# Delta rule of a hybrid block: inverse, u product and state update on four quarters of the array

## The chip, the cores and the metric

The kernel runs as one program on one core of a Trainium2 chip. The metric is the device time in microseconds (us) of one execution; lower is better. Two kernels, before and after one change, are compared. The engines are called as in the profile: PE (TensorE), DVE (VectorE), ACT (ScalarE), POOL (GpSimd) and SP (the queue that issues most DMAs).

## The reference, cut to what matters

The program computes several transformer blocks in one launch. The change lies in one branch of the first block, the gated delta rule, over 256 positions, 4 heads of 128 and chunks of 64 positions:

```python
def gated_deltanet(...):                       # B=1, S=256, H=4, dk=128, C=64, N=4 chunks
    ...
    kb = k * beta[..., None]
    lower = jnp.where(strict, jnp.einsum("bhnid,bhnjd->bhnij", kb, k) * decay, 0.0)
    rhs = jnp.concatenate([v * beta[..., None], kb * jnp.exp(gc)[..., None]], axis=-1)
    sol = lax.linalg.triangular_solve(lower + jnp.eye(C), rhs,
                                      left_side=True, lower=True, unit_diagonal=True)
    u, w = jnp.split(sol, 2, axis=-1)
    ...
    def step(state, xs):
        q_i, k_i, u_i, w_i, a_i, gl_i = xs
        v_new = u_i - jnp.einsum("bhcd,bhde->bhce", w_i, state)
        o_i = jnp.einsum("bhcd,bhde->bhce", q_i, state) + jnp.einsum("bhij,bhje->bhie", a_i, v_new)
        state = state * gl_i[..., None, None] + jnp.einsum("bhcd,bhce->bhde", k_i, v_new)
        return state, o_i
```

So 16 unit lower triangular matrices of 64x64 (4 heads by 4 chunks) are inverted and applied to two right sides, and a scan over the 4 chunks carries a 128x128 state for each head.

## The kernel before, in words

**Weights.** Everything hangs on one stream of weight products. A *unit* is two times 128 rows of a weight matrix, up to 512 columns wide, 512 KB. SP loads it into `raw` (5 slots), ACT writes its high half `whi` (L613), POOL the low half `wlo` (L599), in 6 slots, and PE multiplies it in three f32r products per tile of tokens: a unit of mode "T" (`fv`, `sv`, the gates) is 12 products with 512 columns (recorded at L2127 to L2129), a unit of mode "F" (`su`) is 24 with 256 columns (L2134 to L2137). The order of PE's work is written out by hand. Between pieces of the small branches it calls `from_x(name, start, stop)`, which multiplies some units of the named matrix. The other engines have their own hand-written order and are tied to PE by semaphores. ACT's `high_halves(until)` splits weights up to a unit, `leave(name, ...)` takes a finished product out of PSUM.

**The inverse.** The 16 matrices lie two on top of each other: matrix pair i (0 to 7) is columns 64i to 64i+63, one chunk in partitions 0 to 63 and the next in 64 to 127 (`diag(0)`, `diag(1)`). DVE forms the first approximation from level 0 (the couplings of neighbouring rows), `d_y` = I - masked L, and its transpose `d_x` by blocks. Levels 1 to 5 each couple blocks of twice the size. In a level PE makes t1 = (masked L)(X) for the two halves of the pairs, ACT copies each half from `pm` to `d_t1` (L762), PE multiplies with `d_y`, DVE subtracts the result from `d_x` (L1384) and transposes back into `d_y` (L1387). DVE prepares the masked L of the next levels by `level_mask` (L1360). Each product is 16 fp32 matmuls of 64x64 by 64 columns; the profile shows two records for each. Both operands and the output of one stand in the same half of the partitions, so they use two quarters of the 128x128 array, rows 0 to 63 with columns 0 to 63, and rows 64 to 127 with columns 64 to 127. After each level PE does one weight unit.

**u, w and the scan.** The inverse times `d_vb` gives u, on the same two quarters; `d_kbe` times the inverse gives w, on all four, since its output's half (c) and its operands' (j) run over both. ACT takes u and w out. The scan step n (0 to 3) has: state products (n > 0), a weight piece, v_new on DVE (L1408, L1411), the update of the state on PE (64 rows, 128 columns of the array, n < 3), and after odd n the inner products of both chunks n-1 and n, then another weight piece. DVE takes the update into `d_s` (L1416, L1425).

All small fp32 matmuls of this branch are recorded at the helper `mm`, L2143.

Of the kernel before, what the change touches and what calls it, by code (L numbers as in the profile page):

```python
# [18 lines left out]
ACT = mybir.ActivationFunctionType  # L19
# [154 lines left out]
def const_table():  # L174
# [51 lines left out]
def build(nc, a, out):  # L226
# [8 lines left out]
    with ctx:  # L235
# [192 lines left out]
        d_x, d_y, d_t1, d_mls = dn[:, 10, 0:W], dn[:, 11, 0:W], dn[:, 12, 0:W], (dn[:, 6, 0:W], dn[:, 2, 0:W])  # L428
# [175 lines left out]
        def _(act):  # L604
# [528 lines left out]
        def _(v):  # L1133
# [225 lines left out]
            def level_mask(s):  # L1359
                V.tensor_tensor(by_tile(d_mls[s % 2] if s else d_t1), by_tile(d_lt),  # L1360
                                con(f"lvl{s}").unsqueeze(1).to_broadcast([P, 8, 64]), ALU.mult).then_inc(S["dn_ml"], 1)
            v.wait_ge(S["dn_lt"], 2)
            level_mask(0)
# [10 lines left out]

            v.wait_ge(S["dn_y1"], 1)
            V.transpose(d_x, d_y).then_inc(S["dn_xn"], 1)
            level_mask(1)
            level_mask(2)
            V.tensor_tensor(qT, qT, d_egr, ALU.mult).then_inc(S["dn_y"], 1)
            for s in range(2, 6):  # L1380
                for hf in range(2):
                    half = slice(hf * TOK, (hf + 1) * TOK)
                    v.wait_ge(S["dn_pq"], 2 * (s - 2) + hf + 1)
                    V.tensor_tensor(d_x[:, half], d_x[:, half], pm[:, 2 * hf + 1, 0:TOK], ALU.subtract)\  # L1384
                        .then_inc(S["dn_xn"], 1)
                    v.wait_ge(S["dn_xn"], 4 * (s - 2) + 2 * hf + 2)
                    V.transpose(d_y[:, half], d_x[:, half]).then_inc(S["dn_xn"], 1)  # L1387
                if s < 5:
                    level_mask(s + 1)
                if s == 2:  # L1390
                    v.wait_ge(*evac_at("z"))
                    V.tensor_tensor(zs[:].rearrange("p t (k s) -> p t k s", s=P),
                                    zs[:].rearrange("p t (k s) -> p t k s", s=P),
                                    o_g[:].unsqueeze(1).unsqueeze(1).to_broadcast([P, NT, 4, P]), ALU.mult)
            for hf in range(2):
                half = slice(hf * TOK, (hf + 1) * TOK)
                v.wait_ge(S["dn_pq"], 8 + hf + 1)
                V.tensor_tensor(d_y[:, half], d_y[:, half], pm[:, 2 * hf, 0:TOK], ALU.subtract).then_inc(S["dn_y"], 1)
# [5 lines left out]
            for n in range(4):  # L1404
                t, r = n // 2, 64 * (n % 2)
                if n == 0:
                    v.wait_ge(S["dn_uws"], 1)
                    V.tensor_copy(vn4[r:r + 64, :, t, :], u4[r:r + 64, :, t, :]).then_inc(S["sc_vn"], 1)  # L1408
                else:
                    v.wait_ge(S["sc_ws"], n)  # L1410
                    V.tensor_tensor(vn4[r:r + 64, :, t, :], u4[r:r + 64, :, t, :],  # L1411
                                    pm[r:r + 64, 0, :].rearrange("p (h s) -> p h s", h=4), ALU.subtract)\
                        .then_inc(S["sc_vn"], 1)
# [591 lines left out]
        def _(pe):  # L2005
# [233 lines left out]
            pe.wait_ge(S["dn_vb"], 1)  # L2239
            pe.wait_ge(S["dn_y1"], 1)  # L2240
            def blocks(hf, bank, lhs, rhs):

                for k in range(4):
                    for j in range(2):
                        at = slice(hf * TOK + 64 * k, hf * TOK + 64 * k + 64)
                        last = mm(pm[diag(j), 2 * hf + bank, 64 * k:64 * k + 64], lhs[diag(j), at], rhs[diag(j), at])
                return last
            from_x("fv", 1, 2)
            for s in range(1, 6):
                pe.wait_ge(S["dn_ml"], s + 1)  # L2250
                for hf in range(2):
                    pe.wait_ge(S["dn_xn"], 1 if s == 1 else 4 * (s - 2) + 2 * hf + 2)
                    blocks(hf, 0, d_mls[s % 2], d_x).then_inc(S["dn_t1"], 1)
                for hf in range(2):
                    pe.wait_ge(S["dn_t1c"], 2 * (s - 1) + hf + 1)
                    if s > 1:
                        pe.wait_ge(S["dn_xn"], 4 * (s - 2) + 2 * hf + 3)
                    if s < 5:
                        last = blocks(hf, 1, d_y, d_t1)
                    else:  # L2260
                        last = blocks(hf, 0, d_t1, d_y)
                    last.then_inc(S["dn_pq"], 1)
                from_x(*(("fv", s + 1, s + 2) if s < 3 else ("sv", s - 3, s - 2)))
            pe.wait_ge(S["dn_y"], 3)
            for i in range(8):
                at, cols = slice(64 * i, 64 * i + 64), slice(P * i, P * i + P)
                for j in range(2):
                    mm(flat(P * i)[diag(j)], d_y[diag(j), at], d_vb[diag(j), cols])
            for i in range(8):
                for c in range(2):  # L2270
                    for j in range(2):
                        last = mm(pm[diag(c), 2 + j, 64 * i:64 * i + 64],
                                  d_kbe[diag(j), P * i + 64 * c:P * i + 64 * c + 64],
                                  d_y[diag(j), 64 * i:64 * i + 64])
            last.then_inc(S["dn_uw"], 1)
            from_x("sv", 3, 4)
            from_x("su", 0, 1)

            def swapped(n):

                return pm[diag(1 - n % 2), 1 + n // 2, :]
            for n in range(4):
                t, r = n // 2, 64 * (n % 2)
                rows = slice(r, r + 64)

                def tile(h):
                    return (h * NT + t) * P
                if n:
                    pe.wait_ge(S["sc_s"], n)
                    for h in range(4):  # L2290
                        state = d_s[:, h * P:(h + 1) * P]
                        mm(pm[rows, 0, h * P:(h + 1) * P], d_w[:, tile(h) + r:tile(h) + r + 64], state)
                        last = mm(swapped(n)[:, h * P:(h + 1) * P], qT[:, tile(h) + r:tile(h) + r + 64], state,
                                  start=h == 0, stop=False, skip_group_check=True)
                    last.then_inc(S["sc_ws"], 1)
                    from_x(*(("su", 2, 3), ("gate0_0", 0, 1), ("gate0_0", 2, 3))[n - 1])
                pe.wait_ge(S["sc_vn"], n + 1)
                if n < 3:
                    for h in range(4):
                        i = tile(h)  # L2300
                        last = mm(pm[:, 3, h * P:(h + 1) * P], d_kdec[rows, i:i + P], d_vn[rows, i:i + P])
                    last.then_inc(S["sc_su"], 1)
                if n % 2:
                    for h in range(4):
                        i = tile(h)
                        for m in (n - 1, n):
                            part = diag(m % 2)
                            last = mm(swapped(m)[:, h * P:(h + 1) * P], d_at[part, i // 2:i // 2 + 64],
                                      d_vn[part, i:i + P], start=m == 0 and h == 0, stop=True, skip_group_check=True)
                if n == 3:  # L2310
                    last.then_inc(S["sc_su"], 1)
                from_x(*(("su", 1, 2), ("su", 3, 4), ("gate0_0", 1, 2), ("gate0_0", 3, 4))[n])
            from_x("gate0_1", 0, 3)
            pe.wait_ge(S["dn_o"], 1)
            turn("oa", d_o.rearrange("p (t d) -> p t d", t=NT))
            pe.wait_ge(S["m_cn"], 1)
            turn("cqkv", abc[:, :, 8:8 + 3 * P])
            from_x("gate0_1", 3, 4)
# [540 lines left out]
```

## Time and profile before

| | before |
|---|---|
| median of 3 runs | 1233.92 us (1233.17 to 1234.29) |
| the profiled execution, its own time | 1233.76 us |
| its span, first to last instruction | 1231.9 us |
| PE busy | 1221.6 us (99%) |
| weight loads of PE (PEld) | 1059.9 us (86%) |
| DVE, ACT, POOL busy | 501.2, 661.9, 948.8 us |
| granted TensorE clock | 1.000 |
| DMA | 218.30 MB, 177 GB/s |

The profile records one execution. Busy is the time in which at least one instruction of the engine runs; matmuls overlap, and how many start in a stretch tells more than busy time. The levels of the inverse lie from 104.3 to 130.2 us, u and w to 133.1, the scan from 138.9 to 165.4.

### The profile page before, as it was taken

The page shows a single profiled execution, that of the slowest core. Times are in us where ns is not written, and L with a number is a line of the kernel's source. Part 1 is how long each engine was busy: PE and PEld are TensorE (multiplying, and loading weights), DVE is VectorE, ACT ScalarE, POOL GpSimd, SP SyncE. Part 2 cuts the span into 40 slices and gives each one's busy share as a digit, 9 for nine tenths or more (in the row PEclk, how much of TensorE's full clock was granted, in tenths as well). Part 3 has the DMA queues.
Part 4 walks back from the last instruction along what each step waited for, and adds up shares of the span by engine and source line. Part 5 has one row for each costly group of instructions (what it writes and reads, how often), then busy time and mean ns, then how long its engine had stood idle before and what let it go on. Part 6 is the DMA issues. An engine that isn't in the chain of part 4 may idle for free.

```text
span 1231.9 us, 18271 instructions
## 1 busy us (share of the span) xinstructions
PE 1221.6 (99%) x7389; PEld 1059.9 (86%) x7389; DVE 501.2 (41%) x909; ACT 661.9 (54%) x892; POOL 948.8 (77%) x411
## 2 busy tenths in 40 slices
PE   8999999999999999999999999999999999999998
PEld 7988888888888888899999888888879878888886
DVE  6648346431243300056652153332053674334025
ACT  6774675754467653346444464444445666444433
POOL 7967467739969898767589788889867648998974
PEclk9999999999999999999999999999999999999999
DMA  8745345527756666645466766666638435676652
GB/s 300 210 140 170 90 133 175 167 84 211 216 149 198 188 210 197 183 136 157 130 177 204 251 203 189 189 188 199 199 117 290 140 112 170 190 204 187 211 158 69
DMA packets 147769, 218.30 MB, mean 177 GB/s; under 512 B 9392, under 2 KB 79591, under 8 KB 147687
## 3 DMA queue, kind: packets, MB, share of 16 engines
q1 hardware_dynamic: 144295, 209.92, 56.6%
q10 hardware_dynamic: 3392, 7.23, 1.8%
q8 instruction: 58, 0.95, 0.3%
q14 instruction: 24, 0.20, 0.0%
HBM read 216.08 MB, written 1.05 MB: 176 GB/s over the span
## 4 chain that ended last, share of the span: by engine, by line
PE 92%; DVE 3%; ACT 2%; DMA 1%; issue 1%; POOL 1%; ACTq 0%; POOLq 0%; DVEq 0%
PE acc L2090 18%; PE acc L2127 12%; PE acc L2129 12%; PE acc L2128 12%; PE acc L2097 9%; PE pm L2143 5%; PE acc L2134 4%; PE acc L2136 4%; PE acc L2137 4%; PE acc L2056 2%; PE acc L2057 1%; PE acc L2058 1%; ACT whi L613 1%; PE acc L2342 1%; PE pm L2018 1%
## 5 line engine op out<-in xcount | busy, mean ns | idle before, releaser
L599 POOL TENSOR_TENSOR wlo<-raw,whi 128x1024 fp32r<-128x1024 f32 (+4 forms) x404 | 943.4, 2362 | 271.1 <-ACT whi L613 269.4
L613 ACT ACTIVATE whi<-raw 128x1024 fp32r<-128x1024 f32 (+4 forms) x404 | 411.1, 1036 | 271.9 <-PE acc L2129 135.4
L2090 PE MATMUL acc<-XT,whi 128*128 128x512 f32 x960 | 229.8, 391 | 0.2 <-DVE XT L1171 0.2
L2090 PEld LDWEIGHTS acc<-XT,whi 128*128 128x128 f32 x960 | 176.4, 188 | 34.9 <-issue 0.6
L2097 PEld LDWEIGHTS acc<-XT,wlo 128*128 128x128 f32 x960 | 123.4, 191 | 4.8
L2097 PE MATMUL acc<-XT,wlo 128*128 128x256 f32 x960 | 124.8, 283 | 0.0
L2134 PE MATMUL acc<-XT,whi 128*128 128x256 f32 x432 | 123.3, 285 | 1.4 <-DVE XT L1154 1.4
L2127 PE MATMUL acc<-whi,XT 128*128 128x512 f32 (+4 forms) x320 | 122.6, 383 | 0.1
L2136 PE MATMUL acc<-XT,whi 128*128 128x256 f32 x432 | 122.4, 283 | 0.0
L2137 PE MATMUL acc<-XT,wlo 128*128 128x256 f32 x432 | 122.3, 283 | 0.0
L2129 PE MATMUL acc<-whi,XT 128*128 128x512 f32 (+4 forms) x320 | 119.5, 374 | 0.0
L2128 PE MATMUL acc<-wlo,XT 128*128 128x512 f32 (+4 forms) x320 | 119.5, 373 | 0.0
L2134 PEld LDWEIGHTS acc<-XT,whi 128*128 128x128 f32 x432 | 82.9, 192 | 2.2 <-issue 2.0
L2136 PEld LDWEIGHTS acc<-XT,whi 128*128 128x128 f32 x432 | 83.0, 192 | 0.1
L2137 PEld LDWEIGHTS acc<-XT,wlo 128*128 128x128 f32 x432 | 83.0, 192 | 0.0
L2127 PEld LDWEIGHTS acc<-whi,XT 128*128 128x128 f32 x320 | 60.2, 188 | 11.3 <-issue 1.1
L2129 PEld LDWEIGHTS acc<-whi,XT 128*128 128x128 f32 x320 | 60.2, 188 | 9.9
L2128 PEld LDWEIGHTS acc<-wlo,XT 128*128 128x128 f32 x320 | 60.3, 188 | 9.3 <-issue 0.2
L1762 DVE SCALAR_TENSOR_TENSOR pm<-X,acc 128x512 f32<-128x512 f32 x16 | 10.8, 692 | 108.9 <-PE acc L2129 63.8
L2128 PE MATMUL acc<-wlo,Hhi 128*128 128x512 f32 x136 | 53.0, 389 | 0.0
L2127 PE MATMUL acc<-whi,Hhi 128*128 128x512 f32 x136 | 53.0, 389 | 0.0
L2129 PE MATMUL acc<-whi,Hlo 128*128 128x512 f32 x136 | 52.9, 389 | 0.0
(429 smaller groups left out, 1953.6 us busy)
## 6 DMA issues: line engine op xcount, KB each, us to landing
raw<-in_w_in SPq DMA_DIRECT2D x68, 512.0 KB, 4.1
raw<-in_w_ff SPq DMA_DIRECT2D x64, 512.0 KB, 3.8
raw<-in_w_gate SPq DMA_DIRECT2D x44, 512.0 KB, 3.9
raw<-in_w_up SPq DMA_DIRECT2D x44, 512.0 KB, 3.9
raw<-in_w_down SPq DMA_DIRECT2D x44, 512.0 KB, 4.1
raw<-in_w_in_mix SPq DMA_DIRECT2D x36, 512.0 KB, 4.0
raw<-in_w_branch SPq DMA_DIRECT2D x16, 512.0 KB, 4.0
raw<-in_w_out_mix SPq DMA_DIRECT2D x16, 512.0 KB, 4.3
```

The lines of the kernel that those rows point to most:

```text
L599: nc.gpsimd.tensor_tensor(piece(wlo, u), piece(raw, u), piece(whi, u).bitcast(F32), ALU.subtract).then_inc(S["w_lo"], 1)
L613: return nc.scalar.activation(out_, in_, func, **k)
L2056: T.matmul(o, hi[:, k, tok], wh, start=k == 0 and name not in CONTINUED, stop=False)
L2090: T.matmul(acc[:, n % 2, f, :], piece(whi, u)[:, i, f * P:(f + 1) * P], XT[:, :, k, :], start=k == 0, stop=False)
L2097: last = T.matmul(acc[:, n % 2, f, 0:TOK], piece(wlo, u)[:, i, f * P:(f + 1) * P], XThi[:, k, :], start=False, stop=k == kt - 1)
L2127: T.matmul(o, hi[:, k, tok], wh, start=opens, stop=False)
L2128: T.matmul(o, hi[:, k, tok], wl, start=False, stop=False)
L2129: last = T.matmul(o, lo[:, k, tok], wh, start=False, stop=done)
L2134: T.matmul(o, wh[:, fs], hi[:, k, :], start=opens and f % 2 == 0, stop=False, skip_group_check=True)
L2136: T.matmul(o, wh[:, fs], lo[:, k, :], start=False, stop=False, skip_group_check=True)
L2137: last = T.matmul(o, wl[:, fs], hi[:, k, :], start=False, stop=done, skip_group_check=True)
L2143: return T.matmul(o, lhs, rhs, start=start, stop=stop, **k)
```

## The change

- The masks of levels 1 to 5 change from the upper to the lower blocks. PE multiplies the whole `d_lt` with `d_x`; the mask is applied as DVE takes t1 out of PSUM, one operation on both banks. ACT's ten copies and DVE's `level_mask` calls for levels 1 to 5 go.
- In `blocks`, the back half of the pairs (4 to 7) puts its output into the other half of the partitions (`diag(j ^ hf)`), so the four kinds of matmul use the four quarters. The back half of t1 and of `d_y` is held swapped; `turned_tiles` transposes it in two operations of 64 partitions. The inverse of the back half ends in `d_x`.
- A level is product, half a weight unit (six long matmuls), product, the other half, by the helper `half`, which the kernel already had and which is now defined earlier.
- The u product alternates front and back pairs, the back ones swapped; DVE's `v_new` reads u in two operations.
- The update is cut into two column halves, and the inner product of chunk n-1 stands beside the update of step n; that of chunk 3 stands beside that of 2 at n = 3.
- The multiplication of `zs` moves behind the levels on DVE, the evacuation of `fv` on ACT behind the high halves up to `level_end(3) + AHEAD`.

```diff
@@ const_table @@
-        parts[f"lvl{s}"] = (r // (2 * h) == c // (2 * h)) & ((r // h) % 2 == 0) & ((c // h) % 2 == 1)
+        up = (r // (2 * h) == c // (2 * h)) & ((r // h) % 2 == 0) & ((c // h) % 2 == 1)
+        down = (r // (2 * h) == c // (2 * h)) & ((r // h) % 2 == 1) & ((c // h) % 2 == 0)
+        parts[f"lvl{s}"] = down if s else up
@@ scalar @@
-            high_halves(level_end(0) + AHEAD)
-            for s in range(1, 6):
-                for hf in range(2):
-                    act.wait_ge(S["dn_t1"], 2 * (s - 1) + hf + 1)
-                    cols = slice(hf * TOK, (hf + 1) * TOK)
-                    fn(d_t1[:, cols], pm[:, 2 * hf, 0:TOK], ACT.Copy).then_inc(S["dn_t1c"], 1)
-                high_halves(level_end(s) + AHEAD)
-                if s == 3:
-                    leave("fv", fx[:, :, 2 * W:3 * W])
+            high_halves(level_end(3) + AHEAD)
+            leave("fv", fx[:, :, 2 * W:3 * W])
+            high_halves(level_end(5) + AHEAD)
@@ vector @@
             V.transpose(d_x, d_y).then_inc(S["dn_xn"], 1)
-            level_mask(1)
-            level_mask(2)
+            v.wait_ge(S["dn_xn"], 1)
+            for j in range(2):
+                last = V.transpose(d_y[diag(1 - j), back], d_x[diag(j), back])
+            last.then_inc(S["dn_y1"], 1)
             V.tensor_tensor(qT, qT, d_egr, ALU.mult).then_inc(S["dn_y"], 1)
-            for s in range(2, 6):
...
+            for s in range(1, 6):
+                v.wait_ge(S["dn_t1"], s)
+                V.tensor_tensor(by_tile(d_t1).rearrange("p (a k) s -> p a k s", a=2),
+                                pm[:, 0::2, 0:TOK].rearrange("p a (k s) -> p a k s", s=64),
+                                con(f"lvl{s}").unsqueeze(1).unsqueeze(1).to_broadcast([P, 2, 4, 64]), ALU.mult)\
+                    .then_inc(S["dn_t1c"], 1)
+                v.wait_ge(S["dn_pq"], s)
                 if s < 5:
+                    q, x = two_banks(1, d_x)
+                    V.tensor_tensor(x, x, q, ALU.subtract).then_inc(S["dn_xn"], 1)
+                    v.wait_ge(S["dn_xn"], 2 * s)
+                    turned_tiles(d_y, d_x).then_inc(S["dn_xn"], 1)
+            v.wait_ge(S["dn_xn"], 9)
+            V.tensor_tensor(d_y[:, front], d_y[:, front], pm[:, 1, 0:TOK], ALU.subtract)
+            for j in range(2):
+                last = V.tensor_tensor(d_x[diag(j), back], d_y[diag(1 - j), back], pm[diag(j), 3, 0:TOK], ALU.subtract)
+            last.then_inc(S["dn_y"], 1)
+            v.wait_ge(*evac_at("z"))
...
+                    for hs, j in ((slice(0, 2), n % 2), (slice(2, 4), 1 - n % 2)):
+                        last = V.tensor_tensor(vn4[diag(n % 2), hs, t, :], u4[diag(j), hs, t, :], passed[:, hs, :],
+                                               ALU.subtract)
@@ tensor @@
+            def blocks(bank, lhs, rhs):
+                for k in range(4):
+                    for hf in range(2):
+                        for j in range(2):
+                            at = slice(hf * TOK + 64 * k, hf * TOK + 64 * k + 64)
+                            last = mm(pm[diag(j ^ hf), 2 * hf + bank, 64 * k:64 * k + 64],
+                                      lhs[diag(j), at], rhs[diag(j), at])
+                return last
+            pe.wait_ge(S["dn_vb"], 1)
+            for s in range(1, 6):
+                filler, u = ("fv", s + 1) if s < 3 else ("sv", s - 3)
+                pe.wait_ge(S["dn_xn"], 2 * (s - 1) if s > 1 else 1)
+                blocks(0, d_lt, d_x).then_inc(S["dn_t1"], 1)
+                half(filler, XThi, XTlo, u, 0)
+                pe.wait_ge(S["dn_t1c"], s)
+                pe.wait_ge(*((S["dn_xn"], 2 * s - 1) if s > 1 else (S["dn_y1"], 2)))
+                if s < 5:
+                    last = blocks(1, d_y, d_t1)
+                else:
+                    last = blocks(1, d_t1, d_y)
+                last.then_inc(S["dn_pq"], 1)
+                half(filler, XThi, XTlo, u, 1)
+            pe.wait_ge(S["dn_y"], 2)
...
+            for k in range(4):
+                for i in (k, k + 4):
+                    at, cols = slice(64 * i, 64 * i + 64), slice(P * i, P * i + P)
+                    for j in range(2):
+                        mm(flat(P * i)[diag(j ^ (i // 4))], inverse(i)[diag(j), at], d_vb[diag(j), cols])
...
                 pe.wait_ge(S["sc_vn"], n + 1)
+                def inside(m, h):
+                    part, i = diag(m % 2), (h * NT + m // 2) * P
+                    return mm(swapped(m)[:, h * P:(h + 1) * P], d_at[part, i // 2:i // 2 + 64],
+                              d_vn[part, i:i + P], start=m == 0 and h == 0, stop=True, skip_group_check=True)
+                for h in range(4):
+                    i = tile(h)
+                    if n < 3:
+                        for c in range(2):
+                            last = mm(pm[diag(c), 3, h * P:(h + 1) * P], d_kdec[rows, i + 64 * c:i + 64 * c + 64],
+                                      d_vn[rows, i:i + P])
+                        if h == 3:
+                            last.then_inc(S["sc_su"], 1)
+                    if n:
+                        last = inside(n - 1, h)
+                    if n == 3:
+                        last = inside(n, h)
```

## Rows read from the trace of the kernel before

**Rows 1.** The page, part 1: busy time, share, instructions.

```profile
PE 1221.6 (99%) x7389; PEld 1059.9 (86%) x7389; DVE 501.2 (41%) x909; ACT 661.9 (54%) x892; POOL 948.8 (77%) x411
```

**Rows 2.** Waits of PE, whole span: total us, times, longest.

```profile
PE acc L2134 <- DVE XT L1154: 1.4, 1, 1.4
```

**Rows 3.** Windows: length, busy (count) of PE, PEld, DVE, ACT, POOL, clock, DMA.

```profile
104.30:130.30 26.00, 25.92 (x383) 21.04 (x382) 17.53 (x25) 11.29 (x17) 15.08 (x6) 1.00 0.42 124
```

**Rows 4.** Timeline, level 1: start, duration, instruction [idle before, releaser].

```profile
104.02 0.39 PE L2129 MATMUL acc<-whi,XT 128*128 128x512 f32 x1
104.33 2.31 PE L2143 MATMUL pm<-dn 64*64 64x64 f32 x64
104.41 3.37 DVE L1379 TENSOR_TENSOR dn<-dn 128x1024 f32<-128x1024 f32 x1
105.06 0.85 ACT L613 ACTIVATE dn<-pm 128x256 f32<-128x256 f32 x2 [2.22 <-PE pm L2143]
105.50 1.01 PEld L2143 LDWEIGHTS pm<-dn 64*64 64x64 f32 x32 [0.15 <-ACT dn L613]
...
106.92 0.40 PE L2128 MATMUL acc<-wlo,XT 128*128 128x512 f32 x1
107.15 0.39 PE L2129 MATMUL acc<-whi,XT 128*128 128x512 f32 x1
...
109.52 0.39 PE L2143 MATMUL pm<-dn 64*64 64x64 f32 x6
```

**Rows 5.** Windows, L2143 alone, PE and PEld: level, u, w, state product.

```profile
104.60:105.20 0.60, 0.60 (x28) 0.60 (x24) 1.00 0.58 55
130.70:131.70 1.00, 1.00 (x23) 1.00 (x20) 1.00 0.41 59
132.20:132.80 0.60, 0.60 (x52) 0.60 (x50) 1.00 1.00 389
143.30:143.80 0.50, 0.50 (x14) 0.50 (x12) 1.00 0.41 131
```

**Rows 6.** Timeline, scan: steps n = 0, 1 and 3.

```profile
138.70 0.28 PE L2137 MATMUL acc<-XT,wlo 128*128 128x256 f32 x1
...
140.22 0.28 PE L2136 MATMUL acc<-XT,whi 128*128 128x256 f32 x1
...
146.95 0.28 PE L2137 MATMUL acc<-XT,wlo 128*128 128x256 f32 x1
147.16 2.18 PE L2143 MATMUL pm<-dn 64*128 64x128 f32 x24
...
149.49 0.28 PE L2136 MATMUL acc<-XT,whi 128*128 128x256 f32 x1
149.60 0.29 PE L2137 MATMUL acc<-XT,wlo 128*128 128x256 f32 x1
...
164.03 0.39 PE L2129 MATMUL acc<-whi,XT 128*128 128x512 f32 x1
164.35 1.09 PE L2143 MATMUL pm<-dn 64*64 64x128 f32 x16
165.49 1.02 ACT L613 ACTIVATE dn<-pm 128x1024 f32<-128x1024 f32 x1 [5.09 <-PE pm L2143]
165.71 0.40 PE L2128 MATMUL acc<-wlo,XT 128*128 128x512 f32 x1
```

**Rows 7.** Groups by form, 90 to 133 us: busy us, mean ns, idle before.

```profile
L2143 PEld LDWEIGHTS pm<-dn 64*64 64x64 f32 x416 | 12.9, 134 | 2.9 <-issue 2.1 <-ACT dn L613 0.8
...
L1360 DVE TENSOR_TENSOR dn<-dn,ct 128x512 f32<-128x512 f32 x6 | 11.4, 1921 | 0.0
...
L1387 DVE STREAM_TRANSPOSE dn<-dn 128x256 f32<-128x256 f32 x8 | 3.6, 446 | 0.3
...
L1384 DVE TENSOR_TENSOR dn<-dn,pm 128x256 f32<-128x256 f32 x8 | 3.2, 398 | 3.1 <-PE pm L2143 3.1
...
L1356 DVE TENSOR_TENSOR dn<-pm,ct 128x512 f32<-128x512 f32 x1 | 0.7, 679 | 0.0
```

More of the change, by code:

```diff
@@ L1373, in _, with turned_tiles @@
             V.tensor_tensor(ht(d_vb), vp, heads_of(beta[:]), ALU.mult).then_inc(S["dn_vb"], 1)
+            front, back = slice(0, TOK), slice(TOK, 2 * TOK)
+            def turned_tiles(to, src):
+                V.transpose(to[:, front], src[:, front])
+                for j in range(2):
+                    last = V.transpose(to[diag(1 - j), back], src[diag(j), back])
+                return last
             v.wait_ge(S["dn_y1"], 1)
             V.transpose(d_x, d_y).then_inc(S["dn_xn"], 1)
-            level_mask(1)
@@ L1378, in _ @@
-            level_mask(2)
+            v.wait_ge(S["dn_xn"], 1)
+            for j in range(2):
+                last = V.transpose(d_y[diag(1 - j), back], d_x[diag(j), back])
+            last.then_inc(S["dn_y1"], 1)
             V.tensor_tensor(qT, qT, d_egr, ALU.mult).then_inc(S["dn_y"], 1)
-            for s in range(2, 6):
[L1381 to L1387, printed above, removed]
-                if s < 5:
[L1389 to L1398, printed above, removed]
+            def two_banks(first, ap):
+                return pm[:, first::2, 0:TOK], ap.rearrange("p (a c) -> p a c", a=2)
+            for s in range(1, 6):
[5 more added lines that the diff above has]
+                v.wait_ge(S["dn_pq"], s)
+                if s < 5:
+                    q, x = two_banks(1, d_x)
+                    V.tensor_tensor(x, x, q, ALU.subtract).then_inc(S["dn_xn"], 1)
+                    v.wait_ge(S["dn_xn"], 2 * s)
+                    turned_tiles(d_y, d_x).then_inc(S["dn_xn"], 1)
@@ L1404, in _ @@
             for n in range(4):
-                t, r = n // 2, 64 * (n % 2)
+                t = n // 2
                 if n == 0:
                     v.wait_ge(S["dn_uws"], 1)
-                    V.tensor_copy(vn4[r:r + 64, :, t, :], u4[r:r + 64, :, t, :]).then_inc(S["sc_vn"], 1)
+                    V.tensor_copy(vn4[diag(0), 0:2, t, :], u4[diag(0), 0:2, t, :])
+                    V.tensor_copy(vn4[diag(0), 2:4, t, :], u4[diag(1), 2:4, t, :]).then_inc(S["sc_vn"], 1)
                 else:
                     v.wait_ge(S["sc_ws"], n)
-                    V.tensor_tensor(vn4[r:r + 64, :, t, :], u4[r:r + 64, :, t, :],
-                                    pm[r:r + 64, 0, :].rearrange("p (h s) -> p h s", h=4), ALU.subtract)\
-                        .then_inc(S["sc_vn"], 1)
+                    passed = pm[diag(n % 2), 0, :].rearrange("p (h s) -> p h s", h=4)
+                    for hs, j in ((slice(0, 2), n % 2), (slice(2, 4), 1 - n % 2)):
+                        last = V.tensor_tensor(vn4[diag(n % 2), hs, t, :], u4[diag(j), hs, t, :], passed[:, hs, :],
+                                               ALU.subtract)
+                    last.then_inc(S["sc_vn"], 1)
                 v.wait_ge(S["sc_su"], n + 1)
@@ L2238, in _ @@
             from_x("fv", 0, 1)
[L2239 to L2247, printed above, removed]
-            from_x("fv", 1, 2)
[L2249 to L2318, printed above, removed]
+            from_x("fv", 1, 2)
             def half(name, hi, lo, u, i, used=1):
@@ L2346, in half @@
                     last.then_inc(S["w_used"], used)
+            def blocks(bank, lhs, rhs):
[5 more added lines that the diff above has]
+                                      lhs[diag(j), at], rhs[diag(j), at])
+                return last
+            pe.wait_ge(S["dn_vb"], 1)
@@ new lines, in _, with inverse @@
+            pe.wait_ge(S["dn_y"], 2)
+            def inverse(i):
+                return d_x if i >= 4 else d_y
+            for k in range(4):
+                for i in (k, k + 4):
+                    at, cols = slice(64 * i, 64 * i + 64), slice(P * i, P * i + P)
+                    for j in range(2):
+                        mm(flat(P * i)[diag(j ^ (i // 4))], inverse(i)[diag(j), at], d_vb[diag(j), cols])
+            for i in range(8):
+                for c in range(2):
+                    for j in range(2):
+                        last = mm(pm[diag(c), 2 + j, 64 * i:64 * i + 64],
+                                  d_kbe[diag(j), P * i + 64 * c:P * i + 64 * c + 64],
+                                  inverse(i)[diag(j), 64 * i:64 * i + 64])
@@ new lines, in _, with swapped, tile @@
+            last.then_inc(S["dn_uw"], 1)
+            from_x("sv", 3, 4)
+            from_x("su", 0, 1)
+            def swapped(n):
+                return pm[diag(1 - n % 2), 1 + n // 2, :]
+            for n in range(4):
+                t, r = n // 2, 64 * (n % 2)
+                rows = slice(r, r + 64)
+                def tile(h):
+                    return (h * NT + t) * P
+                if n:
+                    pe.wait_ge(S["sc_s"], n)
+                    for h in range(4):
+                        state = d_s[:, h * P:(h + 1) * P]
+                        mm(pm[rows, 0, h * P:(h + 1) * P], d_w[:, tile(h) + r:tile(h) + r + 64], state)
+                        last = mm(swapped(n)[:, h * P:(h + 1) * P], qT[:, tile(h) + r:tile(h) + r + 64], state,
+                                  start=h == 0, stop=False, skip_group_check=True)
+                    last.then_inc(S["sc_ws"], 1)
+                    from_x(*(("su", 2, 3), ("gate0_0", 0, 1), ("gate0_0", 2, 3))[n - 1])
+                pe.wait_ge(S["sc_vn"], n + 1)
+                def inside(m, h):
+                    part, i = diag(m % 2), (h * NT + m // 2) * P
+                    return mm(swapped(m)[:, h * P:(h + 1) * P], d_at[part, i // 2:i // 2 + 64],
+                              d_vn[part, i:i + P], start=m == 0 and h == 0, stop=True, skip_group_check=True)
+                for h in range(4):
+                    i = tile(h)
+                    if n < 3:
+                        for c in range(2):
+                            last = mm(pm[diag(c), 3, h * P:(h + 1) * P], d_kdec[rows, i + 64 * c:i + 64 * c + 64],
+                                      d_vn[rows, i:i + P])
+                        if h == 3:
+                            last.then_inc(S["sc_su"], 1)
+                    if n:
+                        last = inside(n - 1, h)
+                    if n == 3:
+                        last = inside(n, h)
+                if n == 3:
+                    last.then_inc(S["sc_su"], 1)
+                from_x(*(("su", 1, 2), ("su", 3, 4), ("gate0_0", 1, 2), ("gate0_0", 3, 4))[n])
@@ L2348, in from_branch @@
+            from_x("gate0_1", 0, 3)
+            pe.wait_ge(S["dn_o"], 1)
+            turn("oa", d_o.rearrange("p (t d) -> p t d", t=NT))
+            pe.wait_ge(S["m_cn"], 1)
+            turn("cqkv", abc[:, :, 8:8 + 3 * P])
+            from_x("gate0_1", 3, 4)
             def from_branch(name, start=0, stop=None, ready=None):
```

11 lines of the change are left out of this document (6 added, 5 removed).

## The prediction

> **What bounds the kernel now.** I read the page first: TensorE (PE) is busy for 1221.6 of 1231.9 us [rows 1]. The waits of PE come next: the longest of the whole program is 1.4 us, and none lies between 104 and 166 us, where the delta rule's levels and scan stand [rows 2]. The windows say the same of the levels: from 104.30 to 130.30 us PE is busy 25.92 of 26.00 us at a granted clock of 1.00, while VectorE (DVE) has 17.53, ScalarE (ACT) 11.29 and GpSimd (POOL) 15.08 [rows 3]. So here PE's own stream sets the end. A gain must shorten what PE streams or its switches between forms; work that only moves from ACT to DVE is worth nothing unless PE comes to wait for it.
>
> Last I read the stream itself. Its long products (128x512, f32r) start 0.23 us apart: 106.92, 107.15. A level stands between two of them: the last starts at 104.02, the second after the level at 106.92, so the level costs 2.90 - 2 x 0.23 = 2.44 us [rows 4]. Five levels come 5.19 us apart (104.33, 109.52), each with one unit of 12 long products.
>
> **The price of small products.** Each matmul of 64 rows and 64 columns leaves two records of 0.22 us; how closely they start is read from windows [rows 5]. A window of 0.60 us touches the records that start within 0.60 + 0.22 = 0.82 us. In a level, on the two diagonal quarters, 28 do: 29 ns a record, 58 ns for the pair of quarters. In the w product, which uses all four quarters, 52 do: 16 ns a record, 63 ns for four. The block at 130.3 checks it: u and w begin within 2.63 us; u is 16 pairs at 109 ns (its own row: 23 records of 0.27 in 1.00 + 0.27 us, 55 ns each), 1.74, and leaves 0.89 for w's 16 fours, 56 ns. I take 60 ns for four quarters. So in this trace each quarter keeps its own pace whatever the others do.
>
> A round trip from long products to small ones and back: at 164.03 to 165.71 lie 1.68 - 0.46 = 1.22 us, of which 8 pairs of 128-column records are 0.87; the switch costs 0.35 [rows 6]. The level agrees: 2 products of 16 pairs are 1.86, with 0.35 that is 2.21, and the 0.22 left is the hole between the two, where PE waits for ACT's copy (weights load again at 105.50 [rows 4]).
>
> **Part by part.**
> - *Levels (L2243 to L2263).* The two products of a level go to four quarters: 8 fours at 60 ns, 0.48 us in place of 0.93. Half a unit now lies between them, so each pays its own switch and the hole goes: 2 x (0.48 + 0.35) = 1.66 for 2.44. Five levels: -3.9 us. The units between are the same 5, in halves of six long products: no long product is added or removed.
> - *The u product.* Its 32 records go from 16 pairs to 8 fours at 109 ns: -0.87. The w product is as it was.
> - *Update and inner product.* At n = 0 the update (4 matmuls on 64x128, one at a time) costs 140.22 - 138.70 - 2 x 0.12 = 1.28 us; as 16 records on 64x64 in pairs it is the block at 164.35: 1.22. The same at n = 2, where the inner product of n = 1 is laid on a quarter of the other row half and costs nothing more while the update's two quarters are the longest queues (8 records of 109 ns each). At n = 1 the block now holds the update and then 16 records of inner product, 149.49 - 146.95 - 0.24 = 2.30; afterwards 1.22. At n = 3 nothing changes. Together 0.06 + 1.08 + 0.06: -1.2 [rows 6].
> - *ACT's ten copies of t1 and DVE's five level masks go; DVE gets the masked eviction of t1, a subtract of 512 columns, three transposes.* PE hides these if they fit under half a unit. A block that ends at E = 104.33 + 2.31 = 106.64 has its second long product at E + 0.28, the sixth at E + 1.19, and the next small one 0.31 later: PE is covered for 1.50 us after E [rows 4]. The chain under it: 0.05 to start (the block of 164.35 ends at 165.44, ACT begins at 165.49 [rows 6]), the operation, 0.06 to PE (ACT's first copy ends at 105.44, weights load at 105.50). The masked eviction reads one operand from PSUM and one constant, as L1356 does: 0.68, though the mask between two SBUF tiles, L1360, takes 1.92 on average [rows 7]. Sum 0.79, to spare 0.71. The subtract is L1384 on twice the columns, two of 0.40 at most: 0.91, spare 0.59. The transposes (3 of at most 0.45, L1387) end 0.05 + 0.80 + 0.05 + 1.35 = 2.25 after E; the next level's first product ends at 1.50 + 0.48 + 0.05 + 0.22 = 2.25 and the mask comes 0.05 later. They just fit, and another 0.6 stands behind.
> - *The end of the levels.* Before, the u product had a whole unit over the last subtraction; now it has half, and three operations of 256 columns: 0.05 + 3 x 0.42 + 0.06 = 1.37 under 1.50. This is the thinnest cover; without it each operation costs its 0.42.
> - *The start.* The multiplication of qT by DVE (104.41, 3.37 us [rows 4]) is now queued ahead of the first masked eviction. Two transposes of at most 0.45 precede it in place of two masks of 1.92, so it ends 2.9 us earlier, at 104.8; the first product ends at 104.33 + 0.48 + 0.05 + 0.22 = 105.1.
> - *Moved.* Three things of DVE's queue come behind the levels or beside them: the multiplication of zs after the last subtraction (needed by the output only), and the evacuation of fv on ACT after the high halves of level 3. Both have microseconds to spare. v_new takes two instructions for one, some 0.1 us more, under whole units of 2.7 us or longer. No DMA is added or moved; the high halves of the weights are no longer queued behind ten ACT copies. POOL makes a unit's low half in 15.08 / 6 = 2.5 us, and a level with its unit will take 5.19 - 0.78 = 4.4: supply holds.
>
> Sum: -3.9 - 0.9 - 1.2 = -6.0 us. The profiled execution took 1233.76 (span 1231.9 and 1.86 around it), 0.16 below the median 1233.92. I forecast 1227.8.
>
> **Where a page speaks against it.** The Trainium skill ("TensorE: Matmul & The Clock Gate", section "Wait — 56ns, not 53.3ns?") states a least distance of about 25 ns between starts of matmuls, however small they are. By that a product of 32 records is 0.80 us and not 0.48, a level 2.30, and the whole change gives 0.7 + 0.9 + 1.2 = 2.8 us: 1231.0. The 16 ns a record of w [rows 5] contradict it in this kernel, though only in one burst that followed other small products. Its time lies within the feed rival below; of that rival's chance I give it 0.03.
>
> **The rivals.**
> - *Feed.* The burst of w stood behind u, so its instructions may have been waiting in PE's queue; behind a semaphore, as every product of a level is, they may come no faster than the 29 ns that all level products show (there the two quarters would explain it just as well). Then a product stays 0.93, a level is 2 x 1.28 = 2.56 (+0.6 in all), u gains 0.8 (32 x 29 ns), the scan 1.2: 1232.4. With partial feed it ends between, 1231. This is also the case in which the off-diagonal quarters don't run beside the others. For it: no level shows anything faster. Against: in u and w, and in pairs of column tiles (14 records of 0.27 in 0.50 + 0.27 us), the array's own pace is met exactly.
> - *DVE becomes the bound of the levels: slower.* Place: the eviction and the subtract, one under each half unit. If they are held off by POOL as the masks between SBUF tiles are (1.92 for 0.68 [rows 7]), or by a whole POOL operation of 2.5, a chain of 0.8 to 0.9 becomes 3.3 to 3.4, PE waits 1.85, and ten of them are 18.5 us; POOL works 2.5 of 4.4 us, so some 57% are hit: +10.5 - 6.0, 1238.4. It decides from 0.6 us of wait per chain. Against: L1356, L1384 and L1387 kept 0.68, 0.40 and 0.45 beside POOL.
> - *Weights of one row half load in turn: slower.* Two column tiles on the same rows would then add a load to each four or pair; one load of 64 columns lasts 0.134 us on average [rows 7], though they start 0.03 apart. A level product is then 8 x 0.19 + 0.35 = 1.87, a level 3.74 for 2.44, +6.5 over five; u and the updates +2.3: 1242.6. Against: the pairs of column tiles over all rows run at 55 ns a record, with no room for a load [rows 5]. The Trainium skill, "TensorE: Matmul & The Clock Gate", section "The mechanism" of its part on packing, has this rule: loads overlap running matmuls only where the row group differs.
>
> **How the numbers follow.** Forecast 0.76, own range 1226.8 to 1229.2 (the product at 0.45 to 0.55, the switch 0.30 to 0.40, cover at the end lost once); feed 0.15, spread from 1230.5 to 1232.6; DVE 0.06; loads 0.03. The range 1226.5 to 1231.6 leaves out the two slower cases and a part of feed. A difference under 0.2%, 2.5 us, can't be told from none: faster means under 1231.4. Faster 0.80 (the forecast and a quarter of feed), same 0.12, slower 0.08.
>
> **What would show it.** Right: level blocks of 32 records, starts of the first and the last some 0.5 us apart, two per unit; levels 4.4 us apart; an n = 1 block of some 1.1 us; masked evictions of 0.7; no PE wait for DVE between the levels. A block still 0.93 long means feed; PE or its weight loads waiting on DVE before the second product means the DVE rival. The prediction is wrong if the PE stream shortens by 6 us and the span doesn't, since then something after 166 us, which I take to shift unchanged, gave it back.

## The result

The changed kernel takes 1227.47 us (median of 4 runs, 1227.31 to 1227.80), the kernel before beside it 1233.55 (1233.14 to 1234.29): 6.1 us less, ratio 0.995, 95% interval 0.9938 to 0.9962. The forecast was 1227.8. In the profiled execution the span falls from 1231.9 to 1225.6 us.

The page of the changed kernel, its engines' busy time, and a window over its five levels (columns as in rows 3, with GB/s last):

```profile
PE 1214.7 (99%) x7413; PEld 1052.2 (86%) x7413; DVE 499.1 (41%) x916; ACT 658.6 (54%) x882; POOL 948.0 (77%) x411
```

```profile
104.30:126.60 22.30, 22.30 (x392) 16.23 (x394) 13.30 (x26) 8.03 (x7) 14.24 (x6) 1.00 0.50 144
```

PE is as full as before [rows 1, 3]. It has no fewer matmuls, 24 records more by the halved updates, but it is busy 6.9 us less, because more of them run beside each other. DVE has not become the bound: 13.30 of 22.30 us. The first level, from the timeline of the changed kernel (start, duration, instruction, what it waited for); `mm` is now at L2158, the long products of a half unit at L2278 to L2280:

```profile
103.84 0.39 PE L2144 MATMUL acc<-whi,XT 128*128 128x512 f32 x1
104.16 0.56 PEld L2158 LDWEIGHTS pm<-dn 64*64 64x64 f32 x32 [0.35 <-issue]
104.16 0.69 PE L2158 MATMUL pm<-dn 64*64 64x64 f32 x32
...
104.93 0.69 DVE L1392 TENSOR_TENSOR dn<-pm,ct 128x512 f32<-128x512 f32 x1 [0.52 <-PE pm L2158]
105.13 0.39 PE L2279 MATMUL acc<-wlo,XT 128*128 128x512 f32 x1
...
106.05 0.40 PE L2280 MATMUL acc<-whi,XT 128*128 128x512 f32 x1
106.38 0.56 PEld L2158 LDWEIGHTS pm<-dn 64*64 64x64 f32 x32 [0.37 <-issue]
106.38 0.69 PE L2158 MATMUL pm<-dn 64*64 64x64 f32 x32
...
107.14 0.69 DVE L1399 TENSOR_TENSOR dn<-dn,pm 128x512 f32<-128x512 f32 x1 [1.53 <-PE pm L2158]
...
107.87 0.45 DVE L1373 STREAM_TRANSPOSE dn<-dn 128x256 f32<-128x256 f32 x1
108.32 0.89 DVE L1375 STREAM_TRANSPOSE dn<-dn 64x256 f32<-64x256 f32 x2
108.59 0.69 PE L2158 MATMUL pm<-dn 64*64 64x64 f32 x32
```

Where one block of 64 records took 2.31 us [rows 4], there are two of 32 records, 0.69 us each with the 0.22 of the last record in it. DVE starts on the first product 0.08 us after its end (0.05 expected) and is done well before the next block; the blocks start by PE's own pace ("issue"). From 103.84, the last long product, to 105.13, the second after the block, lie 1.29 us, less 0.46 for the two long ones: 0.83 a product, and 1.66 a level where there were 2.44. Levels come 108.59 - 104.16 = 4.43 us apart, where they came 5.19 apart.

The blocks of u and w, of step n = 1 and of n = 3 in the changed kernel's timeline:

```profile
126.30 2.04 PE L2158 MATMUL pm<-dn 64*64 64x128 f32 x96
128.26 0.50 PE L2142 MATMUL acc<-whi,XT 128*128 128x512 f32 x1
...
142.04 0.28 PE L2152 MATMUL acc<-XT,wlo 128*128 128x256 f32 x1
142.25 1.10 PE L2158 MATMUL pm<-dn 64*64 64x128 f32 x24
...
143.50 0.28 PE L2151 MATMUL acc<-XT,whi 128*128 128x256 f32 x1
...
158.29 1.09 PE L2158 MATMUL pm<-dn 64*64 64x128 f32 x16
159.31 0.50 PE L2142 MATMUL acc<-whi,XT 128*128 128x512 f32 x1
```

The block of u and w ran from 130.27 to the long product at 133.09 before, 2.82 us, and now takes 1.96. The n = 1 block of 24 records took 2.18 us and takes 1.10 [rows 6]. The sum by stage, from first starts in the two profiles:

| stage | before | changed | difference | forecast |
|---|---|---|---|---|
| levels (first small product to u) | 104.33 to 130.27: 25.94 | 104.16 to 126.30: 22.14 | -3.80 | -3.9 |
| u and w | 2.82 | 1.96 | -0.86 | -0.87 |
| scan (to the long product after n = 3) | 133.09 to 165.37: 32.28 | 128.26 to 159.31: 31.05 | -1.23 | -1.2 |
| ahead of the levels | 104.33 | 104.16 | -0.17 | 0 |
| behind the scan (rest of the span) | | | -0.24 | 0 |

The last two rows are in places that the change doesn't touch; I claim nothing from them.

### The profile page after: what moved, and what is told of

It is laid out like the page before. It is cut to its first block, busy times and chain, and to the rows that moved or that the text cites. A ratio compares the mean times of both kernels' runs of the same rounds, so it can differ in the third digit from the quotient of the medians.

```text
span 1225.6 us, 18309 instructions
## 1 busy us (share of the span) xinstructions
PE 1214.7 (99%) x7413; PEld 1052.2 (86%) x7413; DVE 499.1 (41%) x916; ACT 658.6 (54%) x882; POOL 948.0 (77%) x411
## 4 chain that ended last, share of the span: by engine, by line
PE 94%; DVE 2%; ACT 2%; issue 0%; POOL 0%; DMA 0%; POOLq 0%; ACTq 0%; DVEq 0%
PE acc L2105 18%; PE acc L2142 12%; PE acc L2143 12%; PE acc L2144 12%; PE acc L2112 9%; PE pm L2158 5%; PE acc L2149 4%; PE acc L2151 4%; PE acc L2152 4%; PE acc L2071 2%; PE acc L2072 1%; PE acc L2073 1%; PE acc L2278 1%; PE acc L2280 1%; PE acc L2279 1%; PE pm L2033 1%
## 5 line engine op out<-in xcount | busy, mean ns | idle before, releaser
L2142 PE MATMUL acc<-whi,XT 128*128 128x512 f32 (+4 forms) x300 | 114.1, 380 | 0.1
L2144 PE MATMUL acc<-whi,XT 128*128 128x512 f32 (+4 forms) x300 | 111.6, 372 | 0.0
L2143 PE MATMUL acc<-wlo,XT 128*128 128x512 f32 (+4 forms) x300 | 111.6, 372 | 0.0
L2142 PEld LDWEIGHTS acc<-whi,XT 128*128 128x128 f32 x300 | 56.4, 188 | 10.4 <-issue 1.3
L2144 PEld LDWEIGHTS acc<-whi,XT 128*128 128x128 f32 x300 | 56.4, 188 | 9.2
L2143 PEld LDWEIGHTS acc<-wlo,XT 128*128 128x128 f32 x300 | 56.5, 188 | 8.6 <-issue 0.2
L2143 PE MATMUL acc<-wlo,Hhi 128*128 128x512 f32 x136 | 52.9, 389 | 0.0
```

Of the source, the lines that this page charges most:

```text
L2142: T.matmul(o, hi[:, k, tok], wh, start=opens, stop=False)
L2143: T.matmul(o, hi[:, k, tok], wl, start=False, stop=False)
L2144: last = T.matmul(o, lo[:, k, tok], wh, start=False, stop=done)
```

## The experiments

All but the last change one thing in the changed kernel. Times are medians, and the kernel before ran beside each. Two quarters, no half unit, the scan as before and quarters in turn ran in one set, with 1233.70 us for the kernel before; by fours, the mask, half of the cover and the changed kernel again ran in another, with 1234.05. The changed kernel had 1227.47 in the first comparison and 1228.52 in the last set. Ratios are to the kernel before.

**Two quarters.** The back half of the pairs stays in its own partitions.

```diff
-                            last = mm(pm[diag(j ^ hf), 2 * hf + bank, 64 * k:64 * k + 64],
+                            last = mm(pm[diag(j), 2 * hf + bank, 64 * k:64 * k + 64],
...
-                        mm(flat(P * i)[diag(j ^ (i // 4))], inverse(i)[diag(j), at], d_vb[diag(j), cols])
+                        mm(flat(P * i)[diag(j)], inverse(i)[diag(j), at], d_vb[diag(j), cols])
```

(DVE's transposes, last subtraction and reads of u follow, diag(j) for diag(1 - j).)

> The changed kernel with the back half of the pairs left in its own partitions, so that level products and u use two quarters of the array again; half units between, masked eviction and merged update stay. If the four quarters give what I say, each of ten level products takes 0.93 us for 0.47 and u 0.87 more: +5.5 us, 1233.0, a block of 32 records whose first and last starts are 0.92 us apart. Rival: the gain came from the order of the work (no hole, ACT freed, masks gone) and the quarters add little: under 1229.5.

Measured: 1233.30 us, ratio to before 0.9997 (0.9988 to 1.0006): nearly all of the gain is gone. In its profile u and w take 2.83 us again. The scan keeps its 1.2 us, and the levels, 104.35 to 131.01, take 0.7 us more than before. Its first level product in the timeline:

```profile
104.35 1.15 PE L2158 MATMUL pm<-dn 64*64 64x64 f32 x32
105.42 0.50 PE L2278 MATMUL acc<-whi,XT 128*128 128x512 f32 x1
```

The block takes 1.15 us in place of 0.69: 0.46 a product, ten of them 4.6, and u 0.86. The rival, that the new order of the work brings the gain by itself, falls: with two quarters the half unit costs a switch more than the hole that it fills, 2 x (0.93 + 0.35) = 2.56 a level for 2.44.

**No half unit between.** Both halves of the unit stand behind the second product.

```diff
                 blocks(0, d_lt, d_x).then_inc(S["dn_t1"], 1)
-                half(filler, XThi, XTlo, u, 0)
                 pe.wait_ge(S["dn_t1c"], s)
...
                 last.then_inc(S["dn_pq"], 1)
+                half(filler, XThi, XTlo, u, 0)
                 half(filler, XThi, XTlo, u, 1)
```

> The changed kernel with both halves of the unit behind the second product of a level, none between the two products. If the half unit pays by covering DVE's masked eviction, PE now stands still from the end of product 1 for 0.05 + 0.69 + 0.06 = 0.80 us while one switch of 0.35 goes: a level costs 2.27 us for 1.70, +2.9 in all, 1230.4, and the weight loads of product 2 wait on DVE in each level. Rival: a switch of form costs as much as it hides, no change within 0.5 us, 1227.5.

Measured: 1231.13 us, ratio 0.9979 (0.997 to 0.9988): 3.7 us above the changed kernel, for 2.9 expected. Its timeline in level 1 and its waits of PE (total, times, longest):

```profile
104.17 0.69 PE L2158 MATMUL pm<-dn 64*64 64x64 f32 x32
104.93 0.69 DVE L1392 TENSOR_TENSOR dn<-pm,ct 128x512 f32<-128x512 f32 x1 [0.52 <-PE pm L2158]
105.68 0.56 PEld L2158 LDWEIGHTS pm<-dn 64*64 64x64 f32 x32 [0.95 <-DVE dn L1392]
105.68 0.69 PE L2158 MATMUL pm<-dn 64*64 64x64 f32 x32 [0.81 <-DVE dn L1392]
```

```profile
PE pm L2158 <- DVE dn L1392: 4.1, 5, 0.8
```

The hole is 0.81 us as expected, from 104.86 to 105.68. What I had put too low is the level around it: first starts of the two products lie 105.68 - 104.17 = 1.51 apart, 0.69 + 0.82, and from the last long product before to the second behind lie 2.79 us, so the level costs 2.79 - 0.46 = 2.33 and not 2.27; the changed level is 1.66 and not 1.70. 5 x 0.67 is 3.4, and PE's stream at the end of the scan is indeed 3.4 us later than in the changed kernel. The second block here started only when DVE's semaphore came, and it is as short as the others, 0.69 us.

**The scan as before.** Update on 64 rows by 128 columns, then both inner products after odd steps, as in the kernel before (the removed and added lines of the change's last part, turned round).

> The changed kernel with the update and the inner products of the scan as in the kernel before (update on 64 rows by 128 columns, inner products after odd steps). My sum gives the merged form 1.2 us, 1.08 of it at n = 1: 1228.7, the block at n = 1 2.1 us long for 1.1. Rival: the state update waits for the longer block anyway and the later work absorbs it, no change.

Measured: 1229.14 us, ratio 0.9965 (0.9952 to 0.9978), +1.7 by the medians; in the profiled executions the span is 1.2 us longer (1226.8), as PE's stream at the end of the scan is. The block at n = 1:

```profile
142.34 2.17 PE L2158 MATMUL pm<-dn 64*128 64x128 f32 x24
```

The 1.07 us of n = 1 are there (2.17 in place of 1.10), and nothing behind takes them back. The 0.5 by which the medians say more lies inside their interval.

**Quarters in turn, and by fours.** The order of the 16 matmuls of a level product.

```diff
-                for k in range(4):
-                    for hf in range(2):
+                for hf in range(2):
+                    for k in range(4):
                         for j in range(2):
```

> The changed kernel with the matmuls of a level product in another order: the 8 of the front half (diagonal quarters), then the 8 of the back half (the other two). The same quarters, the same work. If PE starts a matmul on a free quarter only when few others stand ahead of it, the two halves run one after the other: 0.87 to 0.93 us a product for 0.47, +4 to +4.7, 1231.7 to 1232.2. If each quarter has a queue of its own that reaches past 8 matmuls, no change, 1227.5.

```diff
-                for k in range(4):
-                    for hf in range(2):
-                        for j in range(2):
+                for k0 in (0, 2):
+                    for hf in range(2):
+                        for k in (k0, k0 + 1):
+                            for j in range(2):
```

> The changed kernel with the matmuls of a level product ordered in runs of four: four on the diagonal quarters, four on the others, twice. With eight in a run the starts took 0.757 us, and the other quarters' first record began while 6 older records had not started. If that is a window of 6 records, a run of 8 records delays the others by one pair of 58 ns: starts over 0.53 to 0.55 us, +0.6 us in all, 1228.1. If instead the other quarters wait for a run to be nearly over whatever its length, 0.64 or more and +1.6 us.

Measured: in turn 1230.71 us (0.9977, 0.9967 to 0.9986); by fours 1227.81 (0.9955, 0.994 to 0.9969). A block in each, from their timelines:

```profile
104.19 0.98 PE L2158 MATMUL pm<-dn 64*64 64x64 f32 x32
```

```profile
105.10 0.74 PE L2158 MATMUL pm<-dn 64*64 64x64 f32 x32
```

In turn, neither of my two theories held: 0.98 lies between 0.69 and the 1.15 of two quarters. It costs 3.2 us by the medians and 2.8 us in PE's stream of the profile. 1.15 - 0.98 = 0.17 is three pairs of 58 ns: for the length of three pairs the two halves run beside each other. How many records have started 0.31 us into a block, counted in windows over the second block, first in turn and then with two quarters:

```profile
106.65:106.99 0.34, 0.31 (x12) 0.31 (x14) 1.00 0.00 0
```

```profile
106.99:107.33 0.34, 0.31 (x10) 0.31 (x12) 1.00 0.06 24
```

Two quarters alone have started 10 by then. In turn there are 12, so the first two of the back half have started while 6 of the 16 records of the front half have not. So PE does start matmuls on a free quarter ahead of older ones, but here not past more than 6 records. Whether that is one window of 6 or a place for 3 on each of the two quarters, both orders would show alike; it stays open.

The size of the delay by fours was put down before that run: 8 records in a run, a window of 6, one pair of 58 ns. The block came out as 0.74 us, 0.05 above the changed kernel's 0.69. Ten products make 0.5 us. That is too little for the timed runs to tell; in the profile, from the first product to the block at n = 3, PE's stream is 54.57 us long (105.10 to 159.67) and the changed kernel's 54.13 (104.16 to 158.29). So the size of the delay came out as the number 6 has it. But it doesn't arise where that sum put it, at the first of the back half: in a window over the block's first 0.05 us (105.05 to 105.15) four records have started, where two quarters alone have started two, so the back half has already begun. Why the later part of the block waits was not followed.

**The mask between SBUF tiles.** DVE copies t1 out of PSUM and masks it in a second operation.

```diff
-                V.tensor_tensor(by_tile(d_t1)..., pm[:, 0::2, 0:TOK]..., con(f"lvl{s}")..., ALU.mult)
+                link(V.tensor_copy(d_e.rearrange("p (a c) -> p a c", a=2), pm[:, 0::2, 0:TOK]))
+                V.tensor_tensor(by_tile(d_t1), by_tile(d_e), con(f"lvl{s}")..., ALU.mult)
```

> The changed kernel with the eviction of t1 in two DVE operations: a copy out of PSUM, then the mask between two SBUF tiles (the form of L1360, 1.92 us on average before). It asks how near the DVE rival was. The half unit covers 1.50 us from the end of the product. If the mask keeps its bare length of 0.69 the chain is 0.05 + 0.69 + 0.05 + 0.69 + 0.06 = 1.54 and nothing is lost (under +0.5 us). If POOL holds it off as it did L1360, the chain is 2.8 us and PE waits 1.3 in each level: +6.4 us, 1234. My account takes the second, with less where POOL stands still at that moment: +3 to +6.5.

Measured: 1238.17 us, ratio 1.0033 (1.0022 to 1.0045): 9.7 above the changed kernel beside it (10.7 above the 1227.47 of the first comparison), and slower than the kernel before. The mask's group by form, PE's wait for it, four windows (columns as above), and the second level in the timeline:

```profile
L1393 DVE TENSOR_TENSOR dn<-dn,ct 128x512 f32<-128x512 f32 x5 | 12.2, 2439 | 0.2
```

```profile
PE pm L2157 <- DVE dn L1393: 8.5, 5, 2.0
```

```profile
110.50:114.40 3.90, 1.92 (x39) 1.28 (x37) 3.19 (x2) 0.24 (x1) 2.36 (x1) 1.00 0.53 141
114.50:117.80 3.30, 3.30 (x26) 2.26 (x30) 2.01 (x4) 0.40 (x1) 0.00 (x0) 0.50 0.44 150
117.90:128.00 10.10, 6.41 (x102) 4.41 (x94) 8.59 (x8) 2.53 (x3) 4.74 (x2) 1.00 0.19 54
128.10:131.50 3.40, 3.40 (x38) 2.64 (x38) 2.01 (x4) 0.00 (x0) 0.00 (x0) 0.50 0.54 159
```

```profile
110.28 0.69 DVE L1392 COPY dn<-pm 128x512 f32<-128x512 f32 x1
110.82 2.36 POOL L601 TENSOR_TENSOR wlo<-raw,whi 128x1024 fp32r<-128x1024 f32 x1 [1.32 <-ACT whi L615]
111.00 2.72 DVE L1393 TENSOR_TENSOR dn<-dn,ct 128x512 f32<-128x512 f32 x1
111.40 0.40 PE L2279 MATMUL acc<-whi,XT 128*128 128x512 f32 x1
113.77 0.69 PE L2157 MATMUL pm<-dn 64*64 64x64 f32 x32 [1.98 <-DVE dn L1393]
```

The direction was mine, the size was not. The masks took 2.44 us each and PE stood 1.7 us in a level, 8.5 in all. The timeline shows what the mask follows: POOL's low half ends at 113.18 and the mask at 113.72, 0.54 later. In the other four levels too it ends some 0.55 us after the low half of POOL that ran when it started, whatever the mask's own length (1.55 to 2.73 us); so did the six masks between SBUF tiles of the kernel before (the one at 109.30 there was 1.28 us long and ended at 110.58, POOL's low half of 106.94 + 3.09 at 110.03). The copy at 110.28 reads PSUM, and the masked eviction of the changed kernel has one operand there; they kept 0.69 us also where POOL's operation ran beside them. Without POOL the mask would have ended near 110.28 + 0.69 + 0.03 + 0.55 = 111.55, an estimate from these rows, and PE by its own pace would have started at 111.40 + 0.32 = 111.72: no wait.

Beyond that the granted clock fell to 0.50, the level of 1.2 GHz, in two stretches of some 3.3 us, behind waits of PE of 1.98 and 1.97 us. PE was busy 49% and 63% of the stretches shown ahead of them. The other three waits, 0.81, 1.73 and 1.99 us, were not followed by such a fall. The long products in the slow stretches start 0.43 us apart in place of 0.23. PE's stream at the block of n = 3 is 170.22 - 158.29 = 11.9 us late in this execution, of 1239.29 us. The seven executions spread from 1236.58 to 1239.59, and the granted clock, averaged over each, goes with them: 1.000 in the shortest, 0.997 in the three longest, 0.998 and 0.999 between. So the waits alone account for 8 to 9 us (1236.58 over the 1228.52 beside it, or over the first 1227.47), and the clock for up to 3 more.

**Half of the cover.** Three long products between the two products of a level, nine behind; `piece_of` is `half` for the token tiles named in its last argument.

```diff
-                half(filler, XThi, XTlo, u, 0)
+                piece_of(filler, u, 0, (0,))
                 pe.wait_ge(S["dn_t1c"], s)
...
-                half(filler, XThi, XTlo, u, 1)
+                piece_of(filler, u, 0, (1,))
+                piece_of(filler, u, 1, (0, 1))
```

> The changed kernel with three long products between the two products of a level in place of six, and nine behind the second. By my chain the masked eviction needs 0.80 us from the end of product 1 and three long products cover 0.83: no wait of PE on DVE, a level costs the same, 1227.5 within 0.5. If the chain is longer than I say (a slack that six products hid), PE waits on DVE before each second product and each 0.1 us costs 0.5 in all.

Measured: 1227.95 us, ratio 0.9951 (0.9936 to 0.9966); no difference from the changed kernel that the runs can tell. Level 1 in its timeline:

```profile
105.91 0.69 DVE L1392 TENSOR_TENSOR dn<-pm,ct 128x512 f32<-128x512 f32 x1 [0.52 <-PE pm L2158]
...
106.34 0.40 PE L2307 MATMUL acc<-whi,XT 128*128 128x512 f32 x1
106.66 0.44 PEld L2158 LDWEIGHTS pm<-dn 64*64 64x64 f32 x24 [0.37 <-DVE dn L1392]
```

DVE ends at 106.60, and weights load at 106.66, 0.32 after the last long product, which is what a switch takes when nothing is waited for [rows 4]. The product ends at 105.14 + 0.69 = 105.83, so the chain from its end to the weight load takes 0.83 us (0.80 expected) and just fits under the 0.83 of three long products; the rest of the half unit's cover is spare for this operation. The wait list names DVE here and yet nothing is lost: it names what came last, not what it cost. From the first product to the block at n = 3 lie 54.16 us (105.14 to 159.30), in the changed kernel 54.13. This kernel and the one by fours reached the levels 1.0 us later in their profiles (105.1), ahead of every line that they change.

**The changed kernel again**, beside by fours, the mask and half of the cover:

> The changed kernel itself, beside the others on their chip: 1227.5, the level product's starts over 0.477 us. It is the base for the three runs beside it.

Measured: 1228.52 us (1227.41 to 1230.64), ratio 0.9957 (0.9942 to 0.9971). Its profiled span agrees with the first one's to 0.1 us (1225.5 and 1225.6); its four executions lie up to 3.2 us apart, those of the first comparison 0.5. So a difference of 1 us between these two sets means nothing.

## Why the prediction was right

- *PE bounds the stretch; only its own stream counts.* Held: the levels, u and the scan gave 5.89 us where 5.97 were summed, and nothing behind 166 us gave them back.
- *Four quarters keep their own pace, also in a burst behind a semaphore.* This was the step that the trace of before could not settle. The two-quarter run and the blocks of 0.69 settle it: 32 records start within 0.69 - 0.22 = 0.47 us, 15 ns each, and they do so too in the run with no half unit between, where the second product really waited for DVE's semaphore. The feed rival falls. The least distance of about 25 ns between matmul starts, which the Trainium skill states ("TensorE: Matmul & The Clock Gate", section "Wait — 56ns, not 53.3ns?"), does not hold for matmuls on different quarters here.
- *A switch costs 0.35 us.* The changed kernel has ten in its levels: 0.83 a product is 0.47 + 0.36. The term 0.48 of the product was 0.01 too high, the switch as much too low.
- *Two column tiles on the same rows load without delay.* Held: the update in pairs takes 1.10 us for 24 records (n = 1), and in the levels 32 loads span 0.56 us. The Trainium skill ("TensorE: Matmul & The Clock Gate", section "The mechanism") states that weight loads overlap running matmuls only where the row group differs. The traces here don't agree: by the prediction's estimate, 8 x 0.19 us, that would have made each block longer than 1.5 us, and it is 0.69.
- *The cover.* 1.50 us against a chain of 0.83: shown by the run with three long products in place of six. The thin place at the end of the levels held too: the last of DVE's three subtractions ends at 126.14, PE starts u at 126.30, 0.32 after its last long product.
- *DVE as the bound, slower.* It did not happen. The run with the mask between SBUF tiles shows that the forecast turned on where this operation reads: the 128x512 multiplication is 0.69 us with one input in PSUM, and 2.44 on average with both in SBUF, because it then ends only some 0.55 us after the running operation of POOL. That my price for this rival (1238.4) lies near what the run measured (1238.2) is luck. I had counted 5.7 chains of 1.85 us, the two kinds of chain and POOL's busy share together; in the run five chains of one kind waited 1.7 us, POOL was busy at the start of all five masks, and the clock, which I had not counted, made up the rest.

## What to carry to other kernels

Read how closely small matmuls start, not how long they last: a place where they already run on all quarters gives the price of the change before it is made. Alternate the quarters matmul by matmul; in runs of 8 they queued behind each other here (0.98 us in place of 0.69), in runs of 4 hardly (0.74). When a product becomes short, the wait for the other engine becomes the larger part: put other PE work between, and let DVE's operation on that chain read one operand from PSUM rather than both from SBUF while POOL works there.

## What the runs showed of the hardware that was not expected

- A matmul may start before older ones that wait for another quarter, past 6 records here and no more: a block is 0.98 us long for runs of 8 matmuls, 0.74 for runs of 4, 0.69 for runs of 2, and 1.15 with two quarters only.
- DVE's multiplication of two SBUF tiles ended some 0.55 us after the POOL operation that ran when it started, in each of the five levels of the mask run (1.55 to 2.73 us long); with one operand in PSUM it took 0.69 us in all five levels of the changed kernel, also inside a POOL operation.
- In the mask run the granted clock fell to 0.50 behind two of the five waits of PE (1.98 and 1.97 us), for some 3.3 us each time; with a wait of 0.81 us in each of the five levels (PE busy 24.93 of 29.00 us) it stayed at 1.00 there.
